# Sums of the up projection's weights made in the first projection, with doubled product banks, another opening and alternating passes

## The reference

```python
h = _rmsnorm(x, lw['g_mix_pre'])
proj = h @ lw['w_in']                       # first projection
...
x = x + _rmsnorm(mix, lw['g_mix_post'])
# _conv_ffn(_rmsnorm(x, g_ffn_pre), ...)
up = h @ w_up                               # (tokens, 2 * D_FF): gates and values
full = jnp.concatenate([prefix.astype(up.dtype), up], axis=1)
conv = b_conv
for j in range(CONV_W):                     # width 3, causal
    conv = conv + full[:, j:j + l] * w_conv[j]
gate, val = jnp.split(conv, 2, axis=-1)
y = (jax.nn.gelu(gate) * val) @ w_down
```

## Time and profile before

| | |
|---|---|
| median of the runs | 2824.97 us |
| profiled execution, own time | 2828.4 us |
| its span, first to last instruction | 2826.7 us |
| PE busy | 2566.1 us (91%) |
| DVE busy | 1549.9 us (55%) |
| ACT busy | 1072.2 us (38%) |
| POOL busy | 1089.0 us (39%) |
| mean granted TensorE clock | 0.957 |
| bytes by DMA | 302.55 MB, 107 GB/s |

### The profile page before, as it was taken

One profiled execution on the slowest core, in us unless ns is written; L12 is line 12 of the kernel. 1 busy time (PEld: TensorE's weight loads), 2 busy tenths in 40 slices (PEclk: granted clock), 3 DMA queues, 4 the chain that ended last, 5 costly groups with the idle time before them and its releaser, 6 DMA issues. The chain is left out here.

```text
span 2826.7 us, 38265 instructions
## 1 busy us (share of the span) xinstructions
PE 2566.1 (91%) x14054; PEld 2292.3 (81%) x14054; DVE 1549.9 (55%) x2063; ACT 1072.2 (38%) x1969; POOL 1089.0 (39%) x1128
## 2 busy tenths in 40 slices
PE   8999999899996888978888968888799999999998
PEld 6789999778775888978888967888778878887887
DVE  4200000588856777898777998777642233334332
ACT  4311111344544544545444544444431232224232
POOL 1100000255545555675555776666400002331222
PEclk9999999899997999988999999999899999999999
DMA  5212122543433332322222323232264457663221
GB/s 170 83 56 68 63 76 73 146 140 125 136 122 101 95 95 88 98 83 82 90 94 82 101 63 94 84 110 80 84 187 117 121 152 233 189 184 107 83 84 41
DMA packets 355248, 302.55 MB, mean 107 GB/s; under 512 B 23528, under 2 KB 306252, under 8 KB 355052
## 3 DMA queue, kind: packets, MB, share of 16 engines
q1 hardware_dynamic: 355090, 300.50, 35.3%
HBM read 223.98 MB, written 76.46 MB: 106 GB/s over the span
## 5 line engine op out<-in xcount | busy, mean ns | idle before, releaser
L2371 DVE SCALAR_TENSOR_TENSOR up_conv<-up_up,ffn_features,up_conv 128x696 f32<-128x696 f32 (+1 forms) x264 | 324.0, 1227 | 144.6 <-ACT up_conv L2219 112.2
L2476 PE MATMUL up_chain<-up_bh,up_ah 128*128 128x348 f32 (+1 forms) x1056 | 354.6, 336 | 26.5 <-ACT up_up L2202 19.1
L2476 PE MATMUL up_chain<-up_bl,up_ah 128*128 128x348 f32 (+1 forms) x1056 | 349.8, 331 | 0.0
L2476 PE MATMUL up_chain<-up_bh,up_al 128*128 128x348 f32 (+1 forms) x1056 | 348.4, 330 | 0.0
L3036 PE MATMUL down_acc<-ple_wh,ple_sh 128*128 128x512 f32 x704 | 276.1, 392 | 17.9 <-DVE ple_wl L2858 14.5
L3036 PE MATMUL down_acc<-ple_wl,ple_sh 128*128 128x512 f32 x704 | 275.4, 391 | 0.0
L3036 PE MATMUL down_acc<-ple_wh,ple_sl 128*128 128x512 f32 x704 | 275.3, 391 | 0.0
L2476 PE MATMUL up_cross<-up_bh,up_ah 128*128 128x348 f32 (+1 forms) x528 | 183.5, 348 | 93.4 <-DVE up_up L2351 82.9
L2307 DVE TENSOR_TENSOR up_al<-up_sums,up_ah 128x512 fp32r<-128x512 f32 x264 | 267.5, 1014 | 0.0
L2107 POOL TENSOR_TENSOR up_conv<-up_conv 128x696 f32<-128x696 f32 (+1 forms) x66 | 133.7, 2026 | 345.1 <-DVE up_conv L2371 245.5
L2032 POOL TENSOR_TENSOR up_sums<-up_raw 128x512 f32<-128x512 f32 x132 | 218.6, 1656 | 81.7 <-DVE up_al L2307 71.3
(11 more groups left out here) (362 smaller groups left out, 6354.7 us busy)
## 6 DMA issues: line engine op xcount, KB each, us to landing
up_raw<-in_w_up SPq DMA_DIRECT2D x132, 512.0 KB, 4.0
lanes<-hidden SPq DMA_DIRECT2D x32, 1408.0 KB, 7.5
hidden<-up_conv SPq DMA_DIRECT2D x44, 348.0 KB, 2.9
proj_features<-in_outs SPq DMA_DIRECT2D x60, 208.0 KB, 1.9
up_x_area<-in_w_down SPq DMA_DIRECT2D x40, 256.0 KB, 5.3
up_x_area<-x SPq DMA_DIRECT2D x18, 512.0 KB, 4.9
in_raw<-in_w_in SPq DMA_DIRECT2D x17, 512.0 KB, 3.9
in_x<-in_x_prompt SPq DMA_DIRECT2D x16, 512.0 KB, 3.8
```

The lines of the kernel that those rows point to most:

```text
L2371: last = nc.vector.scalar_tensor_tensor(out=out[:, 0:n], in0=up[g % 2][kind][:, c:c + n], in1=out[:, 0:n], scalar=taps[:, f, c:c + 1], op0 ...
L2476: last = nc.tensor.matmul(acc[:, 0:HALF[p]], a[:, q % RING, k, :], b[:, m - 1, k, left(p)], start=(opens and k == 0 and i == 0), stop=(k = ...
```

## The change

1. `phase_in` gets the up projection's weights. During its last 13 chunks it loads, 22 times, the gate and value chunk of `w_up` (2 x 512 KB), VectorE makes the four sums (`sums_of_weights`, 4 operations of 128 x 512), and SyncE stores them (1 MB) to a DRAM tensor `weight_sums`. The 22 are spread over 60 of the 65 blocks (`sums_at`).
2. `phase_up` loads the sums it needs from there, 256 KB each, into 6 slots (`SUMS`), and only the half of the value weights that unit 4 uses. GpSimd's weight sums are gone.
3. `cross` and `second` are two banks each; the additional ones are two of the four transposing banks. `five(g)` and `two(g)` wait for step g - 2.
4. The two first steps are interleaved in an opening of their own. Of the four token differences VectorE makes two (`make_t1`, `make_t2`), GpSimd two (`make_t3`, `make_t4`).
5. Pass 2 walks the chunks downwards (`feature`). The last step of a pass and the first of the next then use the same chunk, and its rounded and split weights are kept: 64 sets of weights instead of 66 (`weight_set`, `SETS`).
6. On VectorE and ScalarE the order in a step changes; `scales` moves from the end of the step to before the value taps.

```diff
@@ phase_in, SyncE
+            def load_up(j):
+                if j == 0:
+                    sp.wait_ge(summed, first_bank)
+                for kind in range(2):
+                    sp.dma_start(up_raw[kind][:, :, :], w_up_view[:, :, kind * FF + j * P:kind * FF + (j + 1) * P])\
+                        .then_inc(up_raw_in, 16)
+
+            def store_up(j):
+                sp.wait_ge(up_summed, 4 * j + 4)
+                sp.dma_start(up_sums[j].rearrange("s p n -> p s n"), up_sum[:, :, :, :].rearrange("p s k n -> p s (k n)"))\
+                    .then_inc(up_stored, 16)
...
+                    j = sums_at(n, b)
+                    if j is not None:
+                        store_up(j)
+                        if j + 1 < FC:
+                            load_up(j + 1)
@@ phase_in, VectorE
+            def sums_of_weights(j):
+                gates, values = up_raw
+                dve.wait_ge(up_raw_in, 32 * (j + 1))
+                if j >= 1:
+                    dve.wait_ge(up_stored, 16 * j)
+                nc.vector.tensor_tensor(up_sum[:, 0], values[:, 0:4, :], values[:, 4:8, :], ALU.add).then_inc(up_summed, 1)
...
-            for n in range(4, n_chunks):
+            for n in range(4, wide + 1):
                 split_w(n)
+            for n in range(wide, n_chunks):
+                if n + 1 < n_chunks:
+                    split_w(n + 1)
+                for b in range(NBLK):
+                    j = sums_at(n, b)
+                    if j is not None:
+                        sums_of_weights(j)
@@ phase_up
+def feature(g):
+    return g % FC if pass_of(g) % 2 == 0 else FC - 1 - g % FC
+
+def weight_set(g):
+    return g - pass_of(g)
...
-        chain, first_bank, cross = [bank("chain0"), bank("chain1")], bank("second"), bank("cross")
+        chain = [bank("chain0"), bank("chain1")]
         turn_acc = [bank(f"turn{b}") for b in range(4)]
+        cross, second = [bank("cross"), turn_acc[2]], [bank("second"), turn_acc[3]]
...
+            def load_sum(g, m):
+                i = SUM_PLACES[weight_set(g), m]
+                if i >= SUMS:
+                    sp.wait_ge(a_ready, WEIGHT_PLACES[SUM_ORDER[i - SUMS]] + 1)
+                sp.dma_start(sums[:, i % SUMS], w_sums[feature(g), SUMMED.index(m)].rearrange("p (k n) -> p k n", k=4))\
+                    .then_inc(sums_in[i % SUMS], 16)
...
             def five(g):
-                if g >= 1:
-                    pe.wait_ge(gate_right, g)
-                unit(g, 5, cross, True, False)
+                if g == 1:
+                    pe.wait_ge(laid[0], opening)
+                if g >= 2:
+                    pe.wait_ge(gate_right, g - 1)
+                unit(g, 5, cross[g % 2], True, False)
@@ phase_up, TensorE, opening after two(0)
+            one(1)
+            two(1)
             five(0)
+            five(1)
+            three(0)
+            three(1)
             six(0)
-            three(0)
+            six(1)
             seven(0)
-            for g in range(1, STEPS):
+            seven(1)
+            four(0)
+            four(1)
+            for g in range(2, STEPS):
```

More of the change, by code:

```diff
@@ L148, in phase_in, with sums_at @@
         w_view = w_in.rearrange("(k p) n -> p k n", p=P)
+        w_up_view = w_up.rearrange("(k p) n -> p k n", p=P)
+        def sums_at(n, b):
+            at = (n - wide) * NBLK + b
+            return next((j for j in range(FC) if 60 * (j + 1) // FC == at), None)
         def row_raw(k):
@@ L1876, in turned_tiles, with phase_up @@
     return found
-def phase_up(nc, up_ahead, rows, w_up, gain, taps, bias, prefix, tail, h_scratch, ahead, first_raw, first_in, ident, consts):
+def phase_up(nc, up_ahead, rows, w_up, w_sums, gain, taps, bias, prefix, tail, h_scratch, ahead, first_raw, first_in, ident,
+             consts):
     ctx = ExitStack()
@@ L2250, in _ @@
[L2250 to L2256 removed]
+            lay(0)
+            round_weights(0, 1)
+            lay(1)
+            lay(2)
+            round_block(0, 1)
+            round_weights(0, 2)
@@ L2257, in _ @@
+            round_weights(2, 2)
+            own_tap(1, 1)
+            gelu(0)
+            round_weights(2, 3)
+            round_weights(2, 7)
+            for g in range(2, STEPS):
+                coming = new_weights(g + 1)
+                p, opens, ends = pass_of(g), g % FC == 0, g % FC == FC - 1 and g + 1 < STEPS
                 if opens:
@@ L2391, in _ @@
[L2391 to L2403 removed]
+            scales(2)
@@ new lines, in _ @@
+            lay(0)
+            scales(3)
+            lay(1)
+            split_weights(0, 1)
+            scales(4)
+            lay(2)
+            split_block(0, 1)
+            scales(5)
+            lay(3)
+            split_weights(0, 2)
+            split_block(0, 2)
+            lay(4)
+            lay(5)
+            make_t1(0)
+            split_weights(1, 1)
+            split_block(0, 3)
+            split_weights(1, 2)
+            make_t2(0)
+            split_weights(0, 5)
+            split_block(0, 5)
@@ new lines, in _ @@
+            values_right(0)
+            values_right(1)
+            split_weights(2, 1)
+            split_weights(2, 5)
+            for c in (1, 0):
+                tap(0, 0, c)
+            split_weights(2, 6)
+            split_weights(2, 2)
+            for c in (1, 0):
+                tap(0, 1, c)
+            split_weights(2, 3)
+            split_weights(2, 7)
+            for g in range(2, STEPS):
+                coming = new_weights(g + 1)
+                p, opens, ends = pass_of(g), g % FC == 0, g % FC == FC - 1 and g + 1 < STEPS
+                if g > 2:
@@ L2415, in _ @@
                 if ends:
                     split_block(p + 1, 5)
+                if (g, 4) in coming:
+                    split_weights(g, 4)
+                i = tile_at(g + 1)
+                if i is not None:
+                    scales(i)
+                for c in (1, 0):
+                    tap(g - 1, 1, c)
                 if opens:
                     split_block(p, 4)
-                if g > 0:
-                    tap(g - 1, 1, 1)
-                if g + 1 < STEPS:
-                    split_weights(*ahead_of[2])
@@ L2460, in turns @@
                     for h in range(2):
-                        pe.wait_ge(laid[h], i - 1)
+                        pe.wait_ge(laid[h], i - 1 if i < opening else i)
                 for h in range(2):
@@ L2486, in two @@
             def two(g):
-                if g >= 1:
-                    pe.wait_ge(gate_left, g)
-                unit(g, 2, first_bank, True, True)
+                if g == 1:
+                    pe.wait_ge(laid[1], opening)
+                if g >= 2:
+                    pe.wait_ge(gate_left, g - 1)
+                unit(g, 2, second[g % 2], True, True)
             def three(g):
                 pe.wait_ge(five_kept, g + 1)
-                unit(g, 3, cross, False, True)
+                unit(g, 3, cross[g % 2], False, True)
             def four(g):
```

438 lines of the change are left out of this document (233 added, 205 removed).

## The result

The changed kernel takes **2593.80 us** (median of 4 runs, 2592.89 to 2595.22) against 2824.22 us for the kernel before in the same job: a ratio of 0.9186, 95% interval 0.9170 to 0.9202. The forecast was 2602 us, range 2572 to 2670.

What follows compares the result with a forecast made beforehand. VectorE, slowed under GpSimd's operations, was taken to bound the up stage. Stretches (209.4) with the opening save 225.4 us: 2828.4 - 225.4 + 2 = 2605.0 us profiled, 3.4 over the runs' median, so 2602 us, range 2572 to 2670.

Steps and rivals of the forecast that it cites:

- Stretches: Up stage behind the opening: steps near the 13.41 us floor, 7 us over it per change of pass; saves 209.4 us.
- Opening: First two steps of the up stage, interleaved: 13 units done at 908 instead of 924.12, saving 16 us.
- rule against it: Skill's statement that VectorE and GpSimd share a port pair, held for a whole instruction; prediction saw the trace agreeing in part.
- First projection: Making 22 sums over 60 of its 65 blocks does not reach PE; cost taken as 2 us, between 0 and 44.
- Weight sums: Up stage: GpSimd loses 6.3 us per step; VectorE falls from the bound to 85%, in pass 3 to 89%.
- Banks: Up stage: `five(g)` and `two(g)` wait for step g-2; two us of slack, so PE should not wait in plain steps.
- Scaling moved: Up stage's tile steps: 13 waits of PE, about 5.4 us each, go, and the half clock after each.
- 1 (exclusion as the new bound, 2665): Up stage: VectorE and GpSimd run serially, 14.0 us per plain step and 15.7 in pass 3: 2665 us; chance 0.12.
- 2 (everything hidden): Up stage: changes of pass, tile steps and the 0.2 us per step cost nothing extra: 2574 us; chance 0.08.
- 3: First projection pays after all, 2 us per sum: 2646 us; chance 0.04.
- 4 (half the excess stays): Up stage: something else takes the bank's place; pass 3 and tile steps keep half their excess (31 + 47): 2680 us; chance 0.03.
- 5: Up stage: a slot of the loaded sums comes back too late, kernel slower than before: 2884 us; chance 0.03.

Runs made afterwards that it cites:

- the load: Changed kernel with four unused GpSimd additions of 128x512 put back into each of steps 2 to 65, 5 slots for sums: 2658.58 us, ratio 0.9408.
- the four slots: Changed kernel with 4 slots for the loaded sums instead of 6: 2593.58 us, ratio 0.9179.

## Why the prediction was right, and where not

Right to 0.3%, with errors of both signs in it: the stretches behind the opening saved 20 us more than forecast, the opening 9 less. That the sum is this close is in part luck; without the second error the measured time would have been 17 us off, which is still inside the range.

- **Stretches.** Expected and found savings, in the order of the sum: tiles of pass 1 44.6 and 44.1 (46.1 less the unit of 2.0 us that now lies in the opening), plain steps 5.7 and 3.9 expected, 7.1 and 4.9 found, changes of pass 20.2 and 18.6 against 22.9 and 23.1, tiles of pass 2 49.7 against 54.7, pass 3 62.4 against 68.6, end 4.3 against 3.6. The found ones add up to 229.0 where 209.4 was forecast. Steps lie at the floor, 13.2 in pass 3 instead of 13.5, a step with a tile lies 0.8 above it and not 1.4, and a change of pass 4.9 and 3.1 over three floor steps, not 7.
- **Opening: the step that failed.** "Plus 3 for GpSimd's two remaining differences beside it: 908", 16 us saved. Found: 14 units done at 919.4, so 13 at 917.4: 6.8 saved. The two differences cost 6 us, since each split stood through the whole of one (4.58 and 4.56 instead of 1.6), the first difference could start at 884.5 and not 882.4 (ScalarE's last four copies of a tile), and PE waited in between. This is the exclusion of the "rule against it", which the prediction had weakened to a part. With all four differences on VectorE the 13 units are done at 909.9, near the 908 of the sum.
- **First projection: right, for a margin smaller than said.** "Nothing reaches PE" holds, at the share of 0.75 (0.78 estimated). But the reason given, five output banks against single waits, was not what decides; it is the chain of 11.5 us per sum against 12.2 us of room. The "4.0 us landing, even twice" was near: 7.4 us for 512 KB in this stage.
- **Weight sums: right in their effect, too simple in their cause.** "The long ones lie under GpSimd's operations" is right (splits of sums 761 and 1035 ns without and with the load, those of weights as loaded 947 and 1044, as these lie under the product in both), and the load is worth 65 us. The rest of the sums' part was not VectorE's load but its waits: in pass 3 it was busy for only 251.2 of 318.9 us, which the prediction's own rows said. Copies behind sums in GpSimd's list and taps behind ScalarE's took 3.6 us a step. How much of this the departure of the sums frees and how much the new lists of VectorE and ScalarE, no run here separates: the new lists alone on the kernel before were not tried, and the sums were never taken out of GpSimd without them.
- **Banks: wrong as a cause.** They were put first among the waits; alone they give 4 us on the kernel before (0.15%) and, on the changed one, 1.4 us within the noise by the medians and 3.3 by the traces. The 82.9 us named the handshake that ended last, and the next one, `values_right`, was as late.
- **Scaling moved: right**, and it is the largest single edit on the kernel before, 70 us; on the changed kernel it is 16. The value of the part depends on what stands around it.
- **Rivals.** 1 (exclusion as the new bound, 2665) is out: steps of pass 3 take 13.2 us, not 15.7. Its arithmetic took GpSimd's recorded busy times, which contain waiting, and counted VectorE's sums out of PSUM as excluded, which they are not; that these two make up the difference was not measured. The exclusion itself is real. 2 (everything hidden) is closer to what was found behind the opening than the forecast is: it has 238 us there, the forecast 209.4, found were 229.0. 3 is refuted by PE's 286.67 of 287 us, 4 (half the excess stays) by pass 3 at the floor, 5 by the four slots.

## What to carry to other kernels

Before doubling a buffer for the wait at the top of the list, ask what is late next on the same engine: here the second bank gave 4 us at most with or without the rest, while one line of 1.75 us moved half a step gave 70 us. Work that left an engine paid twice here, by its own time and by what stood behind it in the queue; where the late engine is itself idle for a fifth of the stretch (VectorE here: 251 of 319 us busy), look at the order of its list and of those that it waits for before its load. And work pushed into an idle stage should be costed as a chain (load, compute, store, next load), since here that, and not the bandwidth, set how densely it could be packed.

## What was not expected of the hardware

- VectorE's operation on two SBUF operands stands through the whole of a GpSimd tensor operation that started before it: 4.58 us recorded for work of 1.60 us. With one operand in PSUM it took its usual 0.51 us under such an operation.
- GpSimd's addition of 128x512 has a mean of 1.40 us in the kernel with the load, and single ones take 1.03 us: its records hold waiting for VectorE as well.
- 46 MB more by DMA at 230 GB/s and a share of 0.75 left PE's matmuls in the first projection as they were, 286.67 and 286.73 us busy of 287 with the same count of 1520.
